# A two-block network on one core: feed-forward halves in one block, and retention key blocks that include the meta tokens

## The reference

```
def _swiglu(h, w_gu, w_down):
    gate, up = jnp.split(h @ w_gu, 2, axis=-1)
    return (jax.nn.silu(gate) * up) @ w_down          # width 2816

# retention, 4 heads, 256 wide in q and k, 512 wide in v:
qk = jnp.einsum('bhid,bhjd->bhij', qn, kn).astype(F32) * decay_intra
o = (jnp.einsum('bhij,bhjv->bhiv', qk, vf)
     + jnp.einsum('bhid,bhdv->bhiv', qn.astype(F32) * decay_q[..., None], state))
state = (decay_chunk[:, None, None] * state
         + jnp.einsum('bhjd,bhjv->bhdv', kn.astype(F32) * decay_k[..., None], vf))
...
o = _rms_noaffine(o).reshape(B, T, 2 * D_MODEL).astype(h.dtype)
return (jax.nn.silu(g) * o) @ w_out
```

## Time and profile before

| | us |
|---|---|
| median of 3 runs | 3138.92 (3138.74 to 3140.26) |
| the profiled execution, its own time | 3139.49 |
| its span, first to last instruction | 3137.6 |
| TensorE matmuls busy | 2926.3 (93%) |
| VectorE busy | 1456.8 (46%) |
| ScalarE busy | 1102.9 (35%) |
| mean granted TensorE clock | 0.962 |

### The profile page before, as it was taken

How to read it: one execution, slowest core, us unless ns; L and a number is a source line. 1 busy time by engine, 2 the same in 40 slices (tenths; PEclk the granted TensorE clock), 3 DMA queues, 4 the chain that set the end, 5 groups by cost and what they waited for, 6 DMA issues and landing times. The chain is left out here.

```text
span 3137.6 us, 38874 instructions
## 1 busy us (share of the span) xinstructions
PE 2926.3 (93%) x16104; PEld 2457.6 (78%) x16104; DVE 1456.8 (46%) x1618; ACT 1102.9 (35%) x1505; POOL 86.3 (3%) x89
## 2 busy tenths in 40 slices
PE   5988999999999899999998968899999999899999
PEld 5978999998986578887766767688787787678877
DVE  5474332233513634444476645544445865543322
ACT  3443332222232224331254434333223336444311
POOL 0000000001300000000000010000002000000000
PEclk8989999999999999999999989999999999899999
DMA  3202332322221035555432220355465221033322
GB/s 115 75 28 72 90 94 73 92 91 88 81 81 56 27 91 141 159 155 155 130 93 67 74 48 27 107 159 159 141 184 111 86 94 32 14 94 94 89 83 82
DMA packets 409452, 292.70 MB, mean 93 GB/s; under 512 B 24867, under 2 KB 388196, under 8 KB 409330
## 3 DMA queue, kind: packets, MB, share of 16 engines
q1 hardware_dynamic: 403506, 286.89, 31.5%
q0 software_dynamic: 1600, 3.55, 0.8%
q10 hardware_dynamic: 4224, 0.52, 0.1%
HBM read 286.26 MB, written 4.13 MB: 93 GB/s over the span
## 5 line engine op out<-in xcount | busy, mean ns | idle before, releaser
L197 DVE TENSOR_TENSOR w_lo<-w_raw,w_hi 128x2048 fp32r<-128x2048 f32 (+3 forms) x237 | 499.1, 2106 | 544.7 <-ACT w_hi L191 544.5
L191 ACT ACTIVATE w_hi<-w_raw 128x2048 fp32r<-128x2048 f32 (+3 forms) x237 | 416.0, 1755 | 278.0 <-PE ps L272 176.7
L270 PE MATMUL ps<-ffn_h_hi,w_hi 128*128 128x264 f32 (+1 forms) x1056 | 341.5, 323 | 6.5 <-DVE ffn_h_lo L380 6.5
L272 PE MATMUL ps<-ffn_h_hi,w_lo 128*128 128x264 f32 (+1 forms) x1056 | 340.7, 323 | 0.0
L271 PE MATMUL ps<-ffn_h_lo,w_hi 128*128 128x264 f32 (+1 forms) x1056 | 340.4, 322 | 0.0
L270 PE MATMUL ps<-up_act_hi,w_hi 128*128 128x512 f32 (+1 forms) x880 | 313.1, 356 | 18.1 <-PEq L655 18.1
L271 PE MATMUL ps<-up_act_lo,w_hi 128*128 128x512 f32 (+1 forms) x880 | 311.6, 354 | 0.0
L272 PE MATMUL ps<-up_act_hi,w_lo 128*128 128x512 f32 (+1 forms) x880 | 311.4, 354 | 0.0
L270 PE MATMUL ps<-up_h_hi,w_hi 128*128 128x512 f32 x704 | 279.9, 398 | 7.4 <-DVE up_h_lo L382 7.1
L271 PE MATMUL ps<-up_h_lo,w_hi 128*128 128x512 f32 x704 | 279.7, 397 | 0.0
L272 PE MATMUL ps<-up_h_hi,w_lo 128*128 128x512 f32 x704 | 279.5, 397 | 0.0
(11 more groups left out here) (539 smaller groups left out, 5444.6 us busy)
## 6 DMA issues: line engine op xcount, KB each, us to landing
mod_raw<-in_w_ada_dram SPq DMA_DIRECT2D x128, 384.0 KB, 4.3
w_raw<-in_ffn_w_gu_dram SPq DMA_DIRECT2D x88, 512.0 KB, 5.2
w_raw<-in_w_ffn_in_dram SPq DMA_DIRECT2D x88, 512.0 KB, 5.2
w_raw<-in_ret_w_in_dram SPq DMA_DIRECT2D x24, 1024.0 KB, 5.2
w_raw<-in_ffn_w_down_dram SPq DMA_DIRECT2D x32, 704.0 KB, 5.0
w_raw<-in_w_ffn_out_dram SPq DMA_DIRECT2D x32, 704.0 KB, 5.0
w_raw<-in_dsw_w_in_dram SPq DMA_DIRECT2D x18, 1024.0 KB, 5.1
w_raw<-in_gdn_w_in_dram SPq DMA_DIRECT2D x16, 1024.0 KB, 6.0
```

Of the source, the lines that this page charges most:

```text
L191: self.nc.scalar.activation(self.w_hi[:, s, 0:w.size], self.raw[:, s, 0:w.size], ACT.Copy).then_inc(self.hi_ready, 1)
L197: self.nc.vector.tensor_tensor(self.w_lo[:, s, 0:w.size], self.raw[:, s, 0:w.size], self.w_hi[:, s, 0:w.size].bitcast(F32), ALU.subtract). ...
L270: nc.tensor.matmul(out, w_hi, h_hi, start=first, stop=False)
L272: return nc.tensor.matmul(out, w_lo, h_hi, start=False, stop=last)
```

## The change

**Feed-forward.** The first half becomes a class `Up`, whose engine parts are called inside the block of `add_projected` as its `before`. The end of the block between the halves is gone. On every engine the instructions of the second half follow those of the first. TensorE waits, ahead of the second half's row 0, for the product and the low half of all tiles but the last, and ahead of row 21 for the low half of the last. VectorE waits for its own last low half before it goes on (the sums are cleared in the same space). The first trip of the second half's loop on TensorE stands outside the loop. The order of the loads and of the modulation's work is the same.

**Retention.** Key blocks are now tokens 0 to 127, 128 to 255 and so on of the 528, so the meta tokens lie in the first one. The blocks meet 512, 400, 272 and 144 queries. The 16 tokens that are left over at the end (512 to 527) meet the last 16 queries alone; they are handled in partitions 96 to 111 (`LAST = 96`), with 112 weight columns from token 416 on. The separate decay table of the meta tokens is gone, the other has 528 columns. In `values_and_rotation` the four blocks and the fifth view move likewise.

```diff
 def add_projected(K, w, src, cols, parts=1, base=0, gate=None, side=None, before=None, stats=None):
-        if before:
+        if before and not isinstance(before, Up):
             @block.gpsimd
...
             def first(i, last):
-                trip(i, last, before.row_ready)
+                trip(i, last, before and before.row_ready)
...
-                    if row_ready and j == 0:
+                    if row_ready and j == 0 and parts == 1:
                         for k in range(w.rows):
                             row_ready(pe, k)
                             for m, s in outs:
                                 mm = product(m, s, k)
                     else:
                         for m, s in outs:
                             for k in range(w.rows):
+                                if row_ready and j < parts and (m, s) == outs[0]:
+                                    row_ready(pe, part * w.rows + k)
                                 mm = product(m, s, k)
-            if before:
+            if side is None:
                 K.over_tiles_peeled(pe, w, first, trip)
-            elif side is None:
-                K.over_tiles(pe, w, trip)
             else:
-                K.over_tiles_cut(pe, w, trip, {t: (lambda t=t: side.collapse(pe, 4 + t)) for t in range(4)})
+                first(0, False)
+                side.collapse(pe, 4)
+                K.over_tiles_cut(pe, w, trip, {t: (lambda t=t: side.collapse(pe, 4 + t)) for t in range(1, 4)}, 1)
...
+class Up:      # sync, scalar, vector, tensor hold the first half's loops as they were, and:
+    def vector(self, dve):
...
+        dve.wait_ge(sems["lo"], n["lo"] + up.tiles)
...
+    def row_ready(self, pe, row):
+        if row == 0:
+            pe.wait_ge(self.sems["product"], self.n["product"] + self.up.tiles - 1)
+            pe.wait_ge(self.sems["lo"], self.n["lo"] + self.up.tiles - 1)
+        if row == self.up.tiles - 1:
+            pe.wait_ge(self.sems["lo"], self.n["lo"] + self.up.tiles)
+
+def feed_forward(K, up, down, cols, gate=None, side=None, norm=None, stats=True):
+    with ExitStack() as ctx:
+        first = Up(K, up, cols, norm, side, ctx)
+        add_projected(K, down, (first.a_hi, first.a_lo), cols, parts=2, base=cols[0], gate=gate, side=side,
+                      before=first, stats=Squares(K, cols, first.work) if stats else None)
...
+LAST = 96
 def values_and_rotation(...):
-    views = token_blocks(None, None, 256)[0]
+    views = [(lambda h, c, b=b: h[:, c, b * P:(b + 1) * P], 0, P) for b in range(QB)]
+    views.append((lambda h, c: h[:, c, SEQ - LAST:T], LAST, LAST + N_META))
...
 class RetentionHeads:
+        self.first = [max(0, b * P - N_META) for b in range(QB)]
+        self.pt = [[K.sb("ret_p%d_%d" % (n, b), [P, SEQ - self.first[b]], ctx=ctx) for b in range(QB)] for n in range(2)]
+        self.p_last = K.sb("ret_p_last", [P, 2, N_META], ctx=ctx)
...
-                    mm = nc.tensor.matmul(K.ps[:, b, 0:SEQ - b * P], k[:, c, N_META + b * P:N_META + (b + 1) * P],
-                                          q[:, c, b * P:SEQ], start=d == 0, stop=d == 1)
+                    mm = nc.tensor.matmul(K.ps[:, b, 0:SEQ - self.first[b]], k[:, c, b * P:(b + 1) * P],
+                                          q[:, c, self.first[b]:SEQ], start=d == 0, stop=d == 1)
-                mm = nc.tensor.matmul(K.ps[0:N_META, 4, :], k[:, c, 0:N_META], q[:, c, :], start=d == 0, stop=d == 1)
+                mm = nc.tensor.matmul(K.ps[0:LAST + N_META, 4, 0:N_META], k[:, c, SEQ - LAST:T], q[:, c, SEQ - N_META:SEQ],
+                                      start=d == 0, stop=d == 1)
...
-                nc.tensor.matmul(K.ps[:, bank, :], self.v_meta[:, h * RET_V + m * P:h * RET_V + (m + 1) * P],
-                                 self.pt_meta[:, h % 2, :], start=True, stop=False)
                 for b in range(QB):
-                    mm = nc.tensor.matmul(K.ps[:, bank, b * P:SEQ], v[:, h * QB + b, m * P:(m + 1) * P],
-                                          self.pt[h % 2][b][:], start=False, stop=b == QB - 1)
+                    if b == 1:
+                        nc.tensor.matmul(K.ps[:, bank, SEQ - N_META:SEQ],
+                                         self.v_last[:, h * RET_V + m * P:h * RET_V + (m + 1) * P],
+                                         self.p_last[:, h % 2, :], start=False, stop=False)
+                    mm = nc.tensor.matmul(K.ps[:, bank, self.first[b]:SEQ], v[:, h * QB + b, m * P:(m + 1) * P],
+                                          self.pt[h % 2][b][:], start=b == 0, stop=b == QB - 1)
...
-                    dst, src, by = self.pt_meta[0:N_META, h % 2, :], K.ps[0:N_META, 4, :], self.decay_meta[:, h % 2, :]
+                    rows = slice(LAST, LAST + N_META)
+                    dst, src, by = self.p_last[rows, h % 2, :], K.ps[rows, 4, 0:N_META], self.decay[rows, h % 2, rows]
```

More of the change, by code:

```diff
@@ L634, in add_projected, with __init__ @@
     K.outs_freed += w.tiles // parts
[L637 to L650 removed]
+class Up:
+    def __init__(self, K, up, cols, norm, side, ctx):
+        self.K, self.up, self.cols, self.side = K, up, cols, side
+        W = T - cols[0]
+        self.n = {k: v[1] for k, v in K.up.items()}
+        self.sems = {k: v[0] for k, v in K.up.items()}
+        self.a_hi = K.sb(up.name + "_act_hi", [P, FF_CH, W], F32R, ctx)
+        self.a_lo = K.sb(up.name + "_act_lo", [P, FF_CH, W], F32R, ctx)
+        self.work = K.sb(up.name + "_work", [P, 3 * W], ctx=ctx)
+        self.silu, self.prod = self.work[:, 0:W], self.work[:, W:3 * W].rearrange("p (n w) -> p n w", n=2)
         if side is not None:
@@ L740, in feed_forward, with sync @@
+        self.norm = Normalized(K, cols, gain, shift, side and side.acc[:].rearrange("p n c -> p (n c)"), ctx)
         for k in K.up:
             K.up[k][1] += up.tiles
-        add_projected(K, down, (a_hi, a_lo), cols, parts=2, base=cols[0], gate=gate, side=side,
-                      stats=Squares(K, cols, work) if stats else None)
+    def sync(self, sp):
+        K, up, side = self.K, self.up, self.side
+        if side is None:
+            K.over_tiles(sp, up, lambda i, last: K.loads(sp, up, i, last))
+        else:
+            side.first_loads(sp)
+            K.over_tiles_unrolled(up, lambda i, last: side.loads(sp, up, i, last))
@@ new lines, in tensor, with first, trip, product @@
+    def tensor(self, pe):
+        K, nc, up, sems, n, side = self.K, self.K.nc, self.up, self.sems, self.n, self.side
+        wd = width(self.cols)
+        def first(i, last):
+            trip(i, last, self.norm.chunk_ready)
+        def trip(i, last, chunk_ready=None):
+            for j in range(up.unroll):
+                pe.wait_ge(K.lo_ready, K.tile_no(up, i, j) + 1)
+                pe.wait_ge(sems["product"], i * up.unroll + (n["product"] + j - 1))
+                hi, lo = K.weights(up, j, K.w_hi), K.weights(up, j, K.w_lo)
+                def product(m, s, k):
+                    at = slice(self.cols[0] + s * wd, self.cols[0] + (s + 1) * wd)
+                    return split_products(
+                        nc, K.ps[:, ((j % 2) * 2 + m) * self.cols[1] + s, 0:wd],
+                        hi[:, k, m * P:(m + 1) * P], lo[:, k, m * P:(m + 1) * P],
+                        K.h_hi[:, k, at], K.h_lo[:, k, at], k == 0, k == DC - 1)
+                outs = [(m, s) for m in range(2) for s in range(self.cols[1])]
+                if chunk_ready and j == 0:
+                    for k in range(DC):
+                        chunk_ready(pe, k)
+                        for m, s in outs:
+                            mm = product(m, s, k)
+                else:
+                    for m, s in outs:
+                        for k in range(DC):
+                            mm = product(m, s, k)
+                mm.then_inc(K.tile_used, 1)
+        if side is None:
+            K.over_tiles_peeled(pe, up, first, trip)
+        else:
+            first(0, False)
+            K.over_tiles_cut(pe, up, trip, {t: (lambda g=g: side.collapse(pe, g))
+                                            for g, t in enumerate((2, 4, 7, 9))}, 1)
@@ L1803, in _ @@
                 act.wait_ge(K.tile_used, K.tile_no(w, i, j) + 1)
-                for b, (view, rows) in enumerate(views):
-                    ins = nc.scalar.activation(dest(b, t), place(j, b, rows), ACT.Copy)
+                for b, (view, first, end) in enumerate(views):
+                    ins = nc.scalar.activation(dest(b, t), place(j, b, first, end), ACT.Copy)
                 ins.then_inc(K.psum_free, 1)
@@ L1832, in trip @@
                     hi, lo = K.weights(w, j, K.w_hi), K.weights(w, j, K.w_lo)
-                    for b, (view, rows) in enumerate(views):
+                    for b, (view, first, end) in enumerate(views):
                         for c in range(w.rows):
-                            mm = split_products(nc, place(j, b, P), view(K.h_hi, c), view(K.h_lo, c),
```

(1 more changed line is left out.)

173 lines of the change are left out of this document (52 added, 121 removed).

## The result

The changed kernel takes 3099.32 us (median of four runs, 3096.68 to 3102.04) beside 3139.41 us of the kernel before on the same chip (four runs, 3138.74 to 3140.26): ratio 0.987, with an interval of 0.9856 to 0.9883. That is 40.1 us less; 3100.3 us were predicted. A second comparison (e8) gave 3098.41 us (3098.03 to 3098.58) and a ratio of 0.9868 [0.9853, 0.9883].

What follows compares the result with a forecast made beforehand. TensorE, its matmuls filling 93% of the span, was taken as the bound. From 3139.49 us, 25.8 for the feed-forwards and 12.8 for retention come off: 3100.9, or 3100.3 put on the median; range 3094 to 3109.

Steps and rivals of the forecast that it cites:

- The idle time of the block: Between feed-forward halves: removing the block's end saves 18.1 us of TensorE waits, 18.7 us with 4 x 0.16 added.
- The clock, 7.4 us: Second halves' first tiles ran at granted clock 0.77 to 0.82; without idleness ahead they run at 1.00, saving 7.4 us.
- Stalls of late tiles: Second halves' second and third tiles, margins 0.9 and 0.4 us: 0.15 us of stall each, 1.5 us each at worst.
- Retention, 12.8 us: Retention heads: meta tokens join the key blocks, so the last total comes 12.8 us earlier; bounds 11 to 14.5 us.
- The ring: Retention heads: the loop of reciprocal, gated rows, sums, total and root through all engines sets a 16.8 us period.
- The values stage: Its fifth block takes 112 weight columns in place of 128: nothing gained or lost, bounds -2 to +2 us.
- A: Second halves' first tile waits for the whole first half: 2.9 us four times, 3112 us; with late tiles, chance 0.07.
- B: TensorE stays the bound in retention: 4 us saved in each of four heads, half clock gone, 3097 us; chance 0.05.
- C: Values stage: 112-column weight loads are slow, 21 us over 192 matmuls, giving 3121 us; chance 0.03.
- D: Feed-forwards: the granted clock falls in long unbroken TensorE runs; slower than before, up to 3560 us; chance 0.02.
- E: Whole kernel: nothing measurable changes, as the gaps move to the next shared wait, 3139 us; chance 0.01.
- The term for the rest of the kernel: Elsewhere in the kernel: 2 us either way for half-clock stretches that fall otherwise once everything is shifted.

Runs made afterwards that it cites:

- e8: The changed kernel as it is, measured once more beside the kernel before: 3098.41 us, ratio 0.9868.
- e4: The kernel before, both blocks kept, with useless matmuls filling TensorE's gap behind each first half's last tile: 3133.02 us, ratio 0.9978 to the kernel before.
- e10: The changed kernel with one added 512-column VectorE operation ahead of the second tile's split, in the two feed-forwards with modulation: 3101.84 us, one run.
- e5: The changed kernel with eight added 512-column VectorE operations ahead of the second tile's split, in the two feed-forwards with modulation: 3115.2 us, one run.
- e3: The changed kernel with row 0's wait widened, so the second half waits for the whole first half, still in one block: 3113.87 us, ratio 0.9922.
- e2: The kernel before with only the retention part of the change: 3125.73 us, ratio 0.9959 to the kernel before.
- e6: The changed kernel with VectorE's reciprocal in the retention heads cut from 512 columns to 128: 3095.17 us, one run.

## Why the prediction was right, point by point

**The idle time of the block, 18.7 us: right.** The waits behind L655 are gone, the second halves start 0.12, 0.23, 0.24 and 0.23 us after the last matmul. Taking the modelled end of a matmul out of the sum (4 x 0.16) was right too.

**The clock, 7.4 us: right, and shown.** All four first tiles run at 1.00; e4 got 6.5 us of it with the block in place. The third feed-forward's term was taken over from the second as 2.08 us, where the trace of before has a first tile of 9.61 and a next one of 7.70, 1.91 us apart. The four first tiles together are 7.3 us shorter.

**Stalls of late tiles, 0.3 us: they were 0.** The margins came out at 0.77 and 0.74 us for the second tile (0.9 predicted) and 0.36 and 0.58 for the third (0.4 predicted). e10 and e5 showed that the first is a real margin. Of the third tile's only the trace speaks: no experiment delayed its load. 18.7 + 7.4 = 26.1 us, 25.8 with the stalls taken off, and the four stages gave 26.5.

**Retention, 12.8 us: 13.9.** Output tile 2.46 us, TensorE's price of a head 15.57, first totals 7.5, 10.6 and 11.2 earlier: these terms held. The ring was put at 16.8 for the first two periods, which measured 16.46 and 17.09, and at 18.4 with half clock for the last, which measured 17.23. (The 11.3 us for the third total should have read 11.2 by its own terms.) A step between gated rows takes 2.47 us and not 2.58; against that, in the second period VectorE finished the probabilities before it took up the reciprocal, at 1014.88, while the root was ready at 1014.29. The mis-sized term is the last period: I kept the half clock of before in full and put it at 18.4 us; the two profiled runs of after had 17.23 (clock 0.90), as did e3 and e5, while e2 and e10 had 18.3 and 18.4. This one term, 1.2 us, accounts for the 1.1 us by which the stage was off, since the other two periods' errors cancel (0.3 us each way). Why the half clock lasts longer in some of these runs is open.

**The values stage, nothing: right.** 112.80 us against 113.25. A load of 112 columns took 174 ns, one of 128 took 189, and the matmuls over them took 280 and 281. By the Trainium skill (the page "TensorE: Matmul & The Clock Gate", the section "Weight-path perf modes") only a full 128 columns of a type other than fp32 load fast. Giving up the 128 cost nothing here; no run shows whether these weights ever had a fast load, so the trace neither bears the rule out nor contradicts it.

**The rivals.** A (the wait holds everything) did not occur; built as e3 it costs 14.6 us, not 11.6, in the main because the clock falls in two places of four. B (TensorE the bound in retention) fell by e2 and e6. C (narrow loads) fell by the values stage. D (the clock falls in long runs) fell by 384 us at 1.00. E is out with the result.

**The sum.** 40.4 us came from the places I named, 0.5 us were lost elsewhere, 38.6 were predicted. The term for the rest of the kernel (2 us either way) was needed: three stretches moved by +0.9, +2.8 and -3.0 us, and only their balance was small. It was luck that they balanced. The 1.8 us that the two parts gave beyond the sum are my error; the 0.5 us lost elsewhere hid some of it.

## What to carry to other kernels

Where two loops meet at a barrier, price three things apart: TensorE's idle time, the half clock behind it, and what the first work of the next loop really needs. Here more than half of the feed-forwards' gain (14.6 to 15.8 us of 26.5) needed the third, the wait on single rows. Compute the margin of each later tile from the queue of the engine that prepares it; it is as real as a wait, and the stalls of 2.9 to 4.4 us in e3 and e5 cost up to 2.9 us more through the clock. And where TensorE shortens its own part of a ring, look for the ring: in the heads TensorE had 3.9 us less to do in the first of the three periods and 2.2 us less in the two that hold no scores, and they became shorter by 3.1, 0.6 and 2.7 us (the last with less half clock), and a change of order that opened the ring at its end gave another 6.

## What the runs showed of the hardware that I had not expected

- An idle stretch of 2.9 us ahead of equal work left the clock at 1.00 in two places and took it to 0.83 and 0.82 in two others (e3). What tells them apart is open.
- The stretch at half clock behind the same idleness is not the same from run to run: around the third total of the heads it lasted 3.4 us in after and 6.8 us in e2 and e10, and the period behind it 17.2 against 18.3 and 18.4 us, with the same instructions.
- A small operation of VectorE that waits for its predecessor's result costs 0.66 us where its busy time is 0.48 (e5).
- A fp32 matmul of 16 columns in two passes takes TensorE 0.14 us from its start to the next one's (1014.26 to 1014.40), but the first 400-column pass behind it takes 0.42 us where the second takes 0.34. Together that is the 0.22 us I had put, and the output tile came out at 2.46 as summed.
